# The mixer of layer 0 in a two-layer encoder: streamed convolution weights, movable fold steps, transforms on both sides of the convolution

## The reference

```python
def even_mixer(h, w_in, fourier_w, dw_w, dw_b, gn_g, gn_b, w_out):
    z = h @ w_in                                             # (B, S, 1536)
    u_f = z[..., :FOURIER_WIDTH]                             # 512
    u_val = z[..., FOURIER_WIDTH:FOURIER_WIDTH + CONV_WIDTH] # 512
    u_gate = z[..., FOURIER_WIDTH + CONV_WIDTH:]             # 512
    y_a = fourier_mix(u_f, fourier_w)       # real 2-D DFT per group of 128 channels, then a linear map
    c = u_val * jax.nn.sigmoid(u_gate)
    c = depthwise_conv(c, dw_w) + dw_b      # width 31
    y_b = jax.nn.silu(group_layer_norm(c, gn_g, gn_b))   # 4 groups of 128 channels
    return jnp.concatenate([y_a, y_b], axis=-1) @ w_out
```

## Time and profile before

| | |
|---|---|
| median of 5 runs | 2765.81 us |
| profiled execution | 2766.2 us |
| span of its slowest core (core 0) | 2764.5 us |
| spans of the 8 cores | 2755.8 to 2764.5 us |
| mean granted clock of PE | 0.98 on each core |
| PE busy | 2636.9 us, 95% |
| DVE, ACT, POOL busy | 40%, 38%, 18% |
| the mixer, first projection to output projection | about 505 to 722 us of core 0 |

### The profile page before, as it was taken

How to read it: one execution, slowest core, us unless ns; L and a number is a source line. 1 busy time by engine, 2 the same in 40 slices (tenths; PEclk the granted TensorE clock), 3 DMA queues, 4 the chain that set the end, 5 groups by cost and what they waited for, 6 DMA issues and landing times.

```text
span 2764.5 us, 36632 instructions; the slowest of 8 cores (2755.8 to 2764.5 us)
## 1 busy us (share of the span) xinstructions
PE 2636.9 (95%) x12077; PEld 1205.6 (44%) x12322; DVE 1111.3 (40%) x1631; ACT 1057.7 (38%) x1695; POOL 486.3 (18%) x801
## 2 busy tenths in 40 slices
PE   5999999988799999999999999997999999999997
PEld 1444444433354444444444444443445444444443
DVE  4311721467275641172163135116545665214213
ACT  5312612535577731251252243132127676123112
POOL 1111311214120011121131121110012101112121
PEclk8999999998899999999999999998999999999999
DMA  8554554541462155455455545541235504547568
GB/s 190 90 74 75 81 77 74 89 72 34 75 106 39 20 77 71 75 83 77 71 80 77 75 78 77 72 80 21 35 59 84 87 1 62 77 71 143 76 95 157
DMA packets 120886, 211.19 MB, mean 76 GB/s; under 512 B 14336, under 2 KB 28928, under 8 KB 120704
## 3 DMA queue, kind: packets, MB, share of 16 engines
q0 software_dynamic: 103824, 184.31, 45.3%
q1 hardware_dynamic: 16880, 24.53, 3.1%
HBM read 379.42 MB, written 9.44 MB: 141 GB/s over the span
## 4 chain that ended last, share of the span: by engine, by line
PE 91%; DVE 3%; DMA 2%; issue 2%; ACT 1%; SPq 1%; POOL 0%; DVEq 0%; ACTq 0%; POOLq 0%
PE ps L325 91%; DMA X<-xT 1%; DMA slot<-wflat 1%; DVE FE L990 0%; DVE ET L990 0%; DVE XN L770 0%; DVE BT L1022 0%; SPq L1125 0%; DVE X L814 0%; POOL Y L1079 0%; ACT YP L1117 0%; DVE HO L813 0%; DVE YF L1110 0%; DMA WT<-wt 0%; SPq L691 0%
## 5 line engine op out<-in xcount | busy, mean ns | idle before, releaser
L325 PE MATMUL ps<-XN,slot 128*128 128x512 bf16 x6647 | 1487.7, 382 | 39.4 <-DVE XN L770 23.2
L325 PEld LDWEIGHTS ps<-XN,slot 128*128 128x128 bf16 x6784 | 666.1, 98 | 851.2 <-issue 62.3
L552 POOL DMA_DIRECT2D slot<-wflat x720 | 382.3, 536 | 2151.4 <-PE ps L325 2078.5
L325 PE MATMUL ps<-H,slot 128*128 128x512 bf16 x2761 | 610.3, 379 | 6.4 <-DMA slot<-wflat 3.5
L893 DVE TENSOR_TENSOR H<-ps,s 128x512 bf16<-128x512 f32 x352 | 243.3, 691 | 764.7 <-PE ps L325 626.2
L884 ACT ACTIVATE s<-ps 128x512 f32<-128x512 f32 x352 | 209.8, 597 | 739.1 <-PE ps L325 713.6
L325 PEld LDWEIGHTS ps<-H,slot 128*128 128x128 bf16 x2816 | 275.3, 98 | 336.6 <-issue 5.6
L785 ACT ACTIVATE HO<-ps,cf_sb 128x512 f32<-128x512 f32 x192 | 131.9, 688 | 505.7 <-PE ps L325 498.6
L740 DVE TENSOR_TENSOR acc<-acc,sqd 128x512 f32<-128x512 f32 x80 | 55.4, 692 | 399.9 <-ACT sqd L787 399.8
L770 DVE SCALAR_TENSOR_TENSOR XN<-X,cf_sb,r 128x512 bf16<-128x512 f32 x256 | 181.5, 767 | 47.2 <-ACT r L721 38.5
L813 DVE TENSOR_TENSOR HO<-HO,r 128x512 f32<-128x512 f32 x192 | 129.2, 706 | 130.7 <-ACT r L721 130.6
(11 more groups left out here) (117 smaller groups left out, 1446.5 us busy)
## 6 DMA issues: line engine op xcount, KB each, us to landing
slot<-wflat POOLq DMA_DIRECT2D x648, 256.0 KB, 4.6
slot<-wflat POOLq DMA_DIRECT2D x72, 192.0 KB, 3.8
X<-xT SPq DMA_DIRECT2D x8, 1024.0 KB, 24.2
yT<-X SPq DMA_DIRECT2D x32, 256.0 KB, 6.4
CP<-CR SPq DMA_DIRECT2D x64, 32.0 KB, 3.0
YB<-YP SPq DMA_DIRECT2D x64, 32.0 KB, 1.8
M<-memT SPq DMA_DIRECT2D x1, 1024.0 KB, 26.6
mscr<-MNL SPq DMA_DIRECT2D x2, 512.0 KB, 5.1
```

The costliest lines, as they stand in the source:

```text
L325: self.q["pe"].append((waits, (lambda e: e.matmul(out, lhsT=l_, rhs=r_, start=st, stop=sp)), inc))
L552: self.k.dma("pool", lambda e, dst=dst, src=src: e.dma_start(out=dst, in_=src), "w%d" % idx, cost=1.6, reads=([("X", c, 0) for c in range( ...
```

## The change

- The convolution weights come as 32 panels of the weight stream, two for each block (5 and 4 shifts, 128 x 640 and 128 x 512), in place of WT, the mask and the 16 builds of BT.
- The fold's operations and the clearing of CP's edges become `later` steps, and the `flush` after the projections goes.
- The order of stages becomes: sines of odd 0, four convolution groups each with its tail, cosines of odd 0, sines of odd 1, cosines of odd 1. Their copies and joins become `later` steps.
- In a convolution block YF is copied by ACT or DVE, and Y2 is squared by ACT out of PSUM, where POOL did it from YF. POOL alone multiplies by GR in the first three groups. YF has 12 buffers, not 8, and YP lies in the same place. Ln and Exp follow one another directly. The YB transfers of block 14 are issued by POOL, those of block 15 by ACT.
- `out_proj` has a parameter `early`: with 2, the YA half of the first two column blocks is computed before any YB.
- The planner also counts other engines' readers of a PSUM bank as something that a reader waits for, and holds no bank back. Several tiles move.

```diff
+def conv_block(dw, sg, s0, s1):
+    wt = np.zeros((NPH, 32, s1 - s0, NPH, 32), np.float32)
...
+    for sg in range(NSG):
+        for pc, (s0, s1) in enumerate(((0, SH_A), (SH_A, NSH))):
+            specs.append((("conv", sg, pc), (s1 - s0) * 128,
...
+            if e and k_[0] == "P":
+                for s, v in e[1].items():
+                    if s != eng and need.get(s, 0) < v:
+                        need[s] = v
...
-            self.held = self.held[-1:]
+            self.held = []
...
-    WT = AT(nc, "WT", 72704, [NWT], F32)
     CW = AT(nc, "CW", 75008, [2, 4, 128], BF16)
...
-    YF = [AT(nc, "YF%d" % i, 77824 + i * 2048, [PW], F32) for i in range(8)]
-    BT = [AT(nc, "BT%d" % i, 94208 + i * 3072, [NSH * NPH, 32], BF16) for i in range(4)]
...
+                begun = {}
+                for c in range(early if hf == 0 else 0):
+                    sl = ws.acquire(pkeys_for_c(c))
+                    for tb in tbs:
+                        b = k.bank(reserve=True)
+                        part(b, sl, tb, 0, nk // 2)
+                        begun[(c, tb)] = (b, sl)
...
-            wt, wtk = WT((0, NWT))
-            k.dma("sp", lambda e: e.dma_start(out=wt, in_=wtd), "c2", writes=wtk)
...
             def tt(out, a, b, op, rk, wk):
-                k.op("dve", lambda e: e.tensor_tensor(out=out, in0=a, in1=b, op=op), reads=rk, writes=wk)
+                n = int(np.prod(out.shape[1:]))
+                k.later({"dve": lambda e: e.tensor_tensor(out=out, in0=a, in1=b, op=op)}, reads=rk, writes=wk,
+                        cost={"dve": 0.16 + n * 1.06e-3})
...
-            k.flush()
...
-                if t in (4, 8, 12):
-                    build_bt(t // 4 - 1)
...
+                    w2 = [ws.acquire(("conv", sg, pc)) for pc in range(2)]
                     b = k.bank()
                     pairs = []
                     for sh in range(NSH):
...
+                        w = w2[sh // SH_A]
+                        pairs.append((w.w(sh % SH_A), CP.h[:, sg, sh:sh + PW],
+                                      [w.key] + [cpk(sg, q) for q in range(NPH)] + [("CPPAD",)]))
                     k.mm(P[b][:, :], pairs, b)
...
-                    k.op("act", lambda e, b=b, yf=yf, dwb=dwb: e.activation(out=yf, in_=P[b][:, :], func=AF.Identity, bias=dwb),
-                         reads=[("P", b)] + CONST, writes=yfk)
-                    k.op("pool", lambda e, yf=yf, y2=y2: e.tensor_tensor(out=y2, in0=yf, in1=yf, op=ALU.mult),
-                         reads=yfk, writes=y2k)
...
+                    k.later({"act": lambda e, b=b, y2=y2, dwb=dwb: e.activation(out=y2, in_=P[b][:, :], func=AF.Square, bias=dwb)},
+                            reads=[("P", b)] + CONST, writes=y2k, cost={"act": 0.7})
...
+                        k.later({"pool": mul} if i < 3 else {"dve": mul, "pool": mul}, reads=yfk + grk, writes=yfk)
...
+                        k.later(None, reads=yfk, writes=[ybk(sg)], dma=({14: "pool", 15: "act"}.get(sg, "sp"), fns, "yb%d" % sg))
...
+            sines(0)
+            for i in range(4):
+                conv_tail([conv_group(i)])
+            cosines(0)
+            sines(1)
+            cosines(1)
...
-            out_proj(lambda c: [("lin", "ev_w_out", 0, c)], rhs, 8, l, n_post, False, nxt)
+            out_proj(lambda c: ("lin", "ev_w_out", 0, c), rhs, 8, l, n_post, False, nxt, early=2)
```

## The result

The changed kernel takes 2717.79 us (median of eight executions between 2717.14 and 2718.84), against 2765.81: a ratio of 0.9817 with a 95% interval of 0.9786 to 0.9847. The forecast was 2724 with a range of 2712 to 2745. The profiled execution after took 2718.23 us, and its spans are 2713.0 to 2716.7 us, the slowest being core 6.

What follows compares the result with a forecast made beforehand. PE's matmuls were taken as the bound, so time could come only from PE's gaps and slow clock. Gains of 13.8 (projections), 14.8 (convolution) and 13.1 (way to output projection) sum to 41.7: 2766.2 - 41.7, say 2724 us, range 2712 to 2745.

Steps and rivals of the forecast that it cites:

- The fold: Projections: movable fold steps free the gate product; the 6.4 us wait for CR and slow clock behind it go.
- XN: Projections: without the 4.4 us wait for WT's load, ACT's pre-norm chain starts about 4 to 6 us earlier.
- R2: Rival: first projections keep their loss, XN still late from ACT's table changes; gain 7, not 13.8, 2731 us; chance 0.10.
- a: The mixer's projections, 105.3 us for 403 matmuls: 18.3 lost, 4.5 left, gain 13.8.
- The convolution: Convolution with transforms: builds leave DVE, squares leave POOL; 21.3 us lost, 6.5 left, gain 14.8; ACT nearly full.
- c: The stretch of the convolution with the transforms, 75.3 us before: 21.3 lost, gain 14.8.
- R1: Rival: the convolution waits for its panels, blocks take 3.0 us, not 2.4; 2732 to 2739 us; chance 0.20.
- R3: Rival: the weight queue delivers small panels one behind another, convolution takes 101 us; 2780 us, slower; chance 0.06.
- my 30 of 38 us: Convolution: 4.7 MB of panels at 157 GB/s take 30 us of DMA, beside 38 us of PE.
- The output projection: Way to it after the transforms: PE waits 5.1 to 8 us for YA, YA matmuls cover YB; 8 us left.
- R4: Rival: the last tail is planned so late that YB is again last; +10, 2734 us; chance 0.06.
- d: The 22.6 us stretch before the output projection, 7 matmuls: 21.1 lost, 8 left, gain 13.1.

Runs made afterwards that it cites:

- a_wt: Kernel before, with CW moved 768 bytes up and EX in its old place, so CW leaves the 1024-byte block of WT: 2762.77 and 2765.09 us.
- a_force: Kernel before, with one line making the planner put out pending steps on the upper half of HO at the mixer's start: 2761.72 us.
- u_y2: Changed kernel with the square Y2 put back on POOL, from YF: 2736.95 us.
- a_stream: Kernel before with 32 streamed weight panels in place of the BT builds; squares stay on POOL, old stage order: 2758.15 us.
- g3pool: Changed kernel with all four products with GR of the last group on POOL, where two were on DVE: 2722.18 us.
- u_early: Changed kernel with early = 0, so no YA matmuls go ahead in the output projection: 2724.28 and 2724.76 us.

## Why the prediction was right

- **The fold** was sized well: 6.4 us and slow clock predicted, 8.7 to 9.3 measured. The fold's end cost nothing visible (I had left 1 us): the narrow matmuls start at 594.19 without a wait.
- **XN: the right gain by the wrong cause, which is luck.** The prediction put it down to the load of WT. a_wt shows 2.3 us for that; a_force shows that placing the last post-norm ahead of the mixer's copies on ACT does it, and by the code this came with CP's new place. My step failed where it passed over "several tiles move" at no cost: in this planner a place sets an order, by `claim`. Nor do CW and WT share their place, as I wrote; they meet in one block of 1024 bytes, in which the planner keeps its books. R2 fell with this: a lost 0.4 and 2.4 at the start, less than the 4.5 that I left.
- **The convolution**: 5.7 us lost (59.73 - 54.0), 6.5 predicted. Of the waits, 2.4 are for YH. ACT, which I held for nearly full, was busy 46.20 of 59.73, and u_y2 shows that its squares cost c at most 2.8. DVE was busy 38.02, where I had 28: by its timeline five casts and a product that ran beside POOL's work took some 8 us more there than without it. The small panels landed in 5.2 us, and PE waited for them by at most 0.9 us in a_stream; R1 and R3 fell. But the margin was thinner than my 30 of 38 us, as the last section shows. Of the 16.9 us of c, a_stream shows 8.3; what the new order of the stages and the 12 buffers of YF each add to that was not run.
- **The output projection**: 8 predicted. From 658.13, seven matmuls were done at about 666.8, 7.2 more than their 1.5. YA came as forecast (5.7 in 5.1 to 8), but in part by luck: half of it comes from two products with GR on DVE, which I had not counted there. Without them, in g3pool, the waits are 1.07 + 1.81. The cover of YB came out by two errors against each other: YB landed 20 us after the last statistics, not 14 (the row of u_early puts it at 670.85), and the 16 matmuls ahead took 6.9 us with the lower clock, not 3.5. u_early shows that they hide the 3.71. R4 fell: PE has no wait for YB.
- **The sum**: 41.7 predicted, 46.3 measured in the mean span: 14.2 net in a for 13.8, 30.5 in c and d together for 27.9, 1.1 in the narrow matmuls and 0.5 behind for none. Of the other 1.7 of the 48.0, 1.5 is the smaller spread of the cores.

## What to carry to other kernels

Price the order that a planner makes, not the edit that you read: here a tile's new address reordered ACT's queue, and was worth 5.1 us net beside the 9.3 of the edit that was aimed at the stage. Where a wait is gone in two kernels, undo one part at a time and look which wait comes back; two waits in one stage had two causes. Relief of one engine pays only up to the next late thing: panels alone gave 8 of c's 17 us, and every try to bring YA earlier uncovered YB or was lost behind.

## What the runs showed of the hardware

POOL holds DVE up for longer than one instruction. In the changed kernel a cast that takes 0.42 us without a product of POOL beside it took 4.34, and a product of 0.67 took 3.14. DVE's timeline (first fence) and POOL's (second):

```profile
618.46 0.42 DVE L1101 CAST YH<-YF 128x512 bf16<-128x512 f32 x1
...
621.19 4.34 DVE L1101 CAST YH<-YF 128x512 bf16<-128x512 f32 x1 [0.27 <-ACT YF L1095]
...
646.88 0.43 DVE L1207 TENSOR_TENSOR YA<-ps,SC 128x255 bf16<-128x255 f32 x1
...
656.22 3.14 DVE L1142 TENSOR_TENSOR YF<-YF,GR 128x512 f32<-128x512 f32 x1
...
659.36 0.67 DVE L1142 TENSOR_TENSOR YF<-YF,GR 128x512 f32<-128x512 f32 x1
```
```profile
621.72 2.51 POOL L1142 TENSOR_TENSOR YF<-YF,GR 128x512 f32<-128x512 f32 x2
624.16 1.12 POOL L565 DMA_DIRECT2D slot<-wflat  x2
...
646.22 3.73 POOL L1142 TENSOR_TENSOR YF<-YF,GR 128x512 f32<-128x512 f32 x3
...
656.30 2.50 POOL L1142 TENSOR_TENSOR YF<-YF,GR 128x512 f32<-128x512 f32 x2
```

Both long instructions of DVE end only after POOL has done its second product in a row, and the cast only after POOL's panel issues too; between POOL's two products DVE did not get in. DVE's joins, which read one operand from PSUM, were not held: the row at 646.88 took 0.43 us beside three products of POOL. The Trainium skill, "SBUF — State Buffer", section "SBUF: two separate sides", has an exclusive lock on a shared pair of ports for the whole of one instruction, won by whichever starts first; the trace agrees with the lock, but shows the next POOL instruction going first, though by the profile, where POOL's spans are rough, both DVE instructions had started 0.53 and 0.08 us ahead of POOL's products. Its other half, loads held up by DVE's casts, has no row: two issues on POOL took 1.05 to 1.16 us throughout the convolution.

Loads of half the size are not of half the cost. The weight queue of the changed kernel from 604 to 634 us, where it brought only the convolution's panels (packets, MB, share; KB each, us to landing):

```profile
q0 software_dynamic: 3308, 3.40, 93.9%
...
slot<-wflat POOLq DMA_DIRECT2D x11, 160.0 KB, 5.2
slot<-wflat POOLq DMA_DIRECT2D x11, 128.0 KB, 5.2
```

It moved 3.40 / (0.939 x 30) = 121 GB/s while it worked; with the panels padded to 256 KB it moved 9.48 / (0.932 x 65) = 156, the rate of the earlier trace rows. At 121 GB/s the 4.7 MB of panels take 39 us, not the 30 of the prediction, so the queue had about as much to do as PE's 38. And the small YB transfers landed later beside it; the page after (first fence) and before (second):

```profile
YB<-YP SPq DMA_DIRECT2D x56, 32.0 KB, 5.5
```
```profile
YB<-YP SPq DMA_DIRECT2D x64, 32.0 KB, 1.8
```

That is some 4 of the 6 us by which YB came later than predicted.
